# Decay tiles of the SSD part made during attention, B's convolution off TensorE, carry times decay on POOL

## The reference, cut to what matters

```python
xbc = silu(causal_depthwise_conv(xbc, conv_w, conv_b))       # 4 taps per channel, for x, B and C
xs, Bm, Cm = split(xbc)
a_cs = cumsum(dt * A, axis=2)                                # in chunks of 128 tokens
seg = a_t[..., :, None] - a_t[..., None, :]
decay = exp(where(causal, seg, -inf))                        # (chunk, group, head, 128, 128)
cb = einsum('bclgn,bcsgn->bcgls', Cc, Bc)
y_diag = einsum('bcgrls,bcsgrp->bclgrp', cb * decay, Xdt)
states = einsum('bclgn,bclgr,bclgrp->bcgrpn', Bc, decay_end, Xdt)
def step(carry, inp):                                        # over the chunks
    st, dec = inp
    return carry * dec + st, carry
y_off = einsum('bclgn,bcgrpn,bclgr->bclgrp', Cc, prev, exp(a_cs))
```

## Time and profile before

| | |
|---|---|
| median of 3 runs | 1903.23 us (1896.35 to 1906.76) |
| the profiled execution | 1899.2 us |
| its span, slowest core (7) | 1897.7 us (the cores: 1879.5 to 1897.7) |
| busy PE / DVE / ACT / POOL | 1797.5 / 1128.1 / 741.6 / 595.6 us |
| granted TensorE clock, core 7 | 0.988 |

### The profile page before, as it was taken

How to read it: one execution, slowest core, us unless ns; L and a number is a source line. 1 busy time by engine, 2 the same in 40 slices (tenths; PEclk the granted TensorE clock), 3 DMA queues, 4 the chain that set the end, 5 groups by cost and what they waited for, 6 DMA issues and landing times.

```text
span 1897.7 us, 35295 instructions; the slowest of 8 cores (1879.5 to 1897.7 us)
## 1 busy us (share of the span) xinstructions
PE 1797.5 (95%) x11590; PEld 998.2 (53%) x11590; DVE 1128.1 (59%) x2273; ACT 741.6 (39%) x1818; POOL 595.6 (31%) x730
## 2 busy tenths in 40 slices
PE   5999899999999888999999999999999999999996
PEld 2444455455445455666566656666566654444443
DVE  0134222222222435888988898888989887565565
ACT  1123433433344464555555555555555550000000
POOL 3000000000000103666765666666765660000000
PEclk9999999999999899999999999999999999999999
DMA  9919054441901511463738264453766574444341
GB/s 145 149 22 137 17 90 68 66 84 39 128 17 34 110 37 48 89 115 81 127 81 130 70 113 89 95 113 81 129 162 118 151 236 162 164 146 159 122 134 55
DMA packets 165460, 195.31 MB, mean 103 GB/s; under 512 B 96984, under 2 KB 123768, under 8 KB 158464
## 3 DMA queue, kind: packets, MB, share of 16 engines
q1 hardware_dynamic: 145888, 125.91, 26.1%
q0 software_dynamic: 19392, 67.15, 23.1%
HBM read 213.46 MB, written 42.22 MB: 135 GB/s over the span
## 4 chain that ended last, share of the span: by engine, by line
PE 71%; DVE 11%; DMA 8%; issue 5%; ACT 3%; POOL 1%; SPq 1%; DVEq 0%; ACTq 0%; POOLq 0%
PE bank L347 70%; DMA attst<-atg 3%; DMA vz_slab<-wpack 2%; DVE carry_r L363 2%; DMA slab<-wpack 2%; DVE cv_r L373 1%; DVE MT_r L363 1%; ACT tt L359 1%; ACT P L359 1%; DVE nrw_r L373 1%; DVE yn_r L373 1%; DVE t_r L363 1%; SPq L111 1%; DVE ss_r L368 1%; DVE carry_r L373 1%
## 5 line engine op out<-in xcount | busy, mean ns | idle before, releaser
L347 PE MATMUL bank<-xT_bf,slab 128*128 128x512 bf16 x2048 | 484.5, 382 | 20.6 <-DMA xT_bf<-xT 20.3
L347 PEld LDWEIGHTS bank<-xT_bf,slab 128*128 128x128 bf16 x2048 | 197.2, 99 | 233.2 <-issue 28.8
L347 PE MATMUL bank<-vz_slab,xT_bf 128*128 128x512 bf16 x1024 | 246.8, 384 | 9.2 <-DVE gz L373 6.7
L347 PE MATMUL bank<-w_out_bf,mb 128*128 128x512 bf16 x1024 | 234.7, 382 | 0.0
L347 PE MATMUL bank<-xT_bf,slab_r 128*128 128x512 bf16 x1024 | 234.1, 379 | 0.0
L359 ACT ACTIVATE dec_r<-abc_r,nb_tok 128x128 bf16<-128x128 f32 x512 | 204.7, 400 | 35.7 <-ACT dec_r L359 0.4
L363 POOL TENSOR_TENSOR t_r<-t_r,xd_r 128x256 f32<-128x256 f32 x120 | 102.4, 853 | 276.2 <-DVE t_r L363 274.1
L347 PEld LDWEIGHTS bank<-w_out_bf,mb 128*128 128x128 bf16 x1024 | 100.7, 99 | 122.1 <-issue 5.9
L363 POOL TENSOR_TENSOR abc_r<-abc_r,mask 128x512 f32<-128x512 f32 x128 | 159.8, 1249 | 9.0 <-DMA abc_r<-acs_d 8.4
L347 PEld LDWEIGHTS bank<-vz_slab,xT_bf 128*128 128x128 bf16 x1024 | 98.8, 99 | 116.8 <-issue 16.7
L347 PEld LDWEIGHTS bank<-xT_bf,slab_r 128*128 128x128 bf16 x1024 | 98.1, 98 | 106.7
(11 more groups left out here) (137 smaller groups left out, 2700.5 us busy)
## 6 DMA issues: line engine op xcount, KB each, us to landing
abc_r<-acs_d SPq DMA_DIRECT2D x128, 256.0 KB, 4.1
slab<-wpack POOLq DMA_DIRECT2D x20, 1024.0 KB, 12.7
xt<-x_tok SPq DMA_DIRECT2D x16, 1024.0 KB, 6.2
out<-xt SPq DMA_DIRECT2D x64, 256.0 KB, 2.3
wob<-w_out POOLq DMA_DIRECT2D x24, 512.0 KB, 25.0
slab_r<-wpack POOLq DMA_DIRECT2D x12, 1024.0 KB, 13.6
mb<-mixs SPq DMA_DIRECT2D x16, 768.0 KB, 5.2
xT_bf<-xT POOLq DMA_DIRECT2D x16, 512.0 KB, 44.6
```

The source lines that it names most:

```text
L347: return p.op("pe", lambda e: e.matmul(outap, lhsT, rhs, start=start, stop=stop), reads, writes, signal)
```

## The change

1. **Decay tiles.** From step 62 of the attention stage on, `dec_step` makes one of the 128 decay tiles after another: an SP DMA spreads a row of a_cs over the partitions into `dq` (three buffers), POOL adds the mask, VectorE adds the bias `nb_tok`, ScalarE takes one exponential over 512 columns into `dqo`, and an SP DMA stores it in DRAM (`dec_d`). 107 tiles are made by step 240, the rest by about step 312. The load of tile m + 3 follows the exponential of tile m. In the SSD stage `load_dec` brings each tile back four chunks ahead, into four buffers; `abc`, its masks and the four exponentials of `front` are gone.
2. **B's convolution.** For all blocks but the first, `conv_ew(2)` takes the place of `conv_fm(2)`: as C's, with one ScalarE and three VectorE instructions, issued within `proj(0)`. Both copies of `uT` that VectorE made (j = 0 and 2) go to ScalarE.
3. **Carry.** The product of carry and decay moves from VectorE, ahead of the addition, to POOL, behind the cast `prev_bf`, for the next chunk.
4. **Room.** `attst` has two buffers and not three; the new tiles lie on `dt_tok`, on the constants (`ones_bf` is set after step 256 by a memset) and on unused halves of `tt`.

```diff
@@ in the attention stage
+        def dq_of(i):
+            return i % 3 if i % 3 < 2 or i < DQ_TURN else 3
+        def dec_load(i):
             if i < 128:
+                k = dq_of(i)
+                p.dma("sp", [(dq[k][:, :], acs_d[i // 16, i % 16].rearrange("h l -> (h l)")
+                              .unsqueeze(0).to_broadcast([128, 512]))], "dq%d" % k, reads=[b_acsd], writes=[b_dq[k]])
+        def dec_add(i):
+            if i < 128:
+                k, g, c = dq_of(i), i // 16, i % 16
+                v = dq[k][:, :].rearrange("p (a b) -> p a b", a=4)
+                TT("pool", dq[k][:, :], dq[k][:, :], mask4_bf[:, :], ALU.add, [b_const], [b_dq[k]])
+                TT("dve", v, v, nb_tok[:, c, 4 * g:4 * g + 4].unsqueeze(2).to_broadcast([128, 4, 128]), ALU.add,
+                   [b_ssdc], [b_dq[k]])
+        def dec_out(i):
+            return i % 2 + (2 if i >= DQ_LAST else 0)
+        def dec_exp(i):
+            k, o_ = dq_of(i), dec_out(i)
+            ACT(dqo[o_][:, :], dq[k][:, :], AF.Exp, [b_dq[k]], [b_dqo[o_]])
+        def dec_store(i):
+            o_ = dec_out(i)
+            p.dma("sp", [(dec_d[i], dqo[o_][:, :])], "dqs%d" % o_, reads=[b_dqo[o_]], writes=[b_decd[i]])
...
+        DQ_START, DQ_LAST = 62, 107
+            goal = (i - DQ_START) * DQ_LAST // (240 - DQ_START) if i < 240 else DQ_LAST + (i - 240) * (128 - DQ_LAST) // 72
+            while ndq[0] < min(128, goal):
+                m = ndq[0]
+                ndq[0] += 1
+                dec_exp(m)
+                dec_store(m)
+                dec_load(m + 3)
+                dec_add(m + 1)
...
             E_act(i)
             if i % 2 == 1 and i < 60:
                 next(dtgen, None)
+            dec_step(i)
@@ SSD stage: gen_A
-                CPY("dve" if j % 2 == 0 else "act", uT[:, j, 3:515], banks[bk][:, :], [bkb[bk]], [b_uT[j]])
+                CPY("act", uT[:, j, 3:515], banks[bk][:, :], [bkb[bk]], [b_uT[j]])
...
-            yield from proj(0)
-            yield from conv_fm(2)
+            for i_, v in enumerate(proj(0)):
+                if i_ == 0 and Q > 0:
+                    conv_ew(2, cv2, b_cv2, BT[par][:, :], [b_BT[par]])
+                yield v
+            if Q == 0:
+                yield from conv_fm(2)
@@ front
             ACT(cb_bf[i2][:, :], banks[0][:, 0:128], AF.Copy, [bkb[0]], [b_cb[i2]], scale=0.25)
-            for hl in range(4):
-                ACT(dec_bf[i2][:, hl * 128:(hl + 1) * 128], abc[i3][:, hl * 128:(hl + 1) * 128], AF.Exp,
-                    [b_abc[i3], b_ssdc], [b_dec[i2]], bias=nb_tok[:, c, 4 * g + hl:4 * g + hl + 1])
@@ back_ew
-            if 0 < c < 15:
-                TT("dve", v4(carry[:, :]), v4(carry[:, :]), bc4(cd_bc[:, hs4, c]), ALU.mult, [b_ssdc], [b_carry])
...
             if c < 15:
                 CPY("act", prev_bf[:, :], carry[:, :], [b_carry], [b_prev])
+            if c < 14:
+                TT("pool", v4(carry[:, :]), v4(carry[:, :]), bc4(cd_bc[:, hs4, c + 1]), ALU.mult, [b_ssdc], [b_carry])
@@ the loop over n
-                load_abc(n + 5)
-                mask_abc(n + 3)
+                load_dec(n + 4)
                 back_ew(n)
```

More of the change, by code:

```diff
@@ L286, in make_cpack @@
     put("convbg", cbg)
-    cbc = np.zeros((128, 8, 5), np.float32)
-    for g in range(8):
-        ch = 3072 + g * 128 + np.arange(128)
-        cbc[:, g, 0:4] = conv_w[:, ch].T
-        cbc[:, g, 4] = conv_b[ch]
-    put("convbc", cbc.reshape(128, 40))
+    cbc = np.zeros((128, 2, 8, 5), np.float32)
+    for b in range(2):
+        for g in range(8):
+            ch = 3072 - 1024 * b + g * 128 + np.arange(128)
+            cbc[:, b, g, 0:4] = conv_w[:, ch].T
+            cbc[:, b, g, 4] = conv_b[ch]
+    put("convbc", cbc.reshape(128, 80))
     return cp
@@ L329, in build_program @@
     b_acsd = Buf("acs_d")
+    dec_d = nc.dram_tensor("dec_d", [128, 128, 512], BF16, kind="Internal").ap()
+    b_decd = [Buf("dec_d%d" % i) for i in range(128)]
     tot_d = nc.dram_tensor("tot_d", [32, 16], F32, kind="Internal").ap()
@@ L765, in build_program @@
         gz_tok = [RB.alloc([128, 4, 256], BF16, "gz_tok%d" % i) for i in range(2)]
-        abc = [RE.alloc([128, 512], F32, "abc%d" % i) for i in range(4)]
+        dec_bf = [RE.alloc([128, 512], BF16, "dec%d" % i) for i in range(4)]
+        dq.append(RE.alloc([128, 512], F32, "dq3"))
+        dqo += [RE.alloc([128, 512], BF16, "dqo%d" % i) for i in (2, 3)]
+        b_dq.append(Buf("dq3"))
         normw = [RA.alloc([128, 256], F32, "normw0"), RD1.alloc([128, 256], F32, "normw1")]
@@ L1326, in O_st @@
         def O_st(h, g):
-            a3 = (4 * h + g) % 3
+            a3 = (4 * h + g) % 2
             bm = Buf("mix")
```

103 lines of the change are left out of this document (64 added, 39 removed).

## The result

The kernel got slower. The changed kernel took 1930.8 to 1936.2 us, the kernel before 1896.35 to 1906.76; the ratio is 1.0165, 95% interval 1.0122 to 1.0207. Three of its six executions came in a slower state, in which the cores of one die show a lower granted clock; such executions are left out of every time and ratio in this document. The forecast was 1878, range 1850 to 1908: wrong, and on the wrong side. The profiled execution took 1930.96, its span 1929.4 against 1897.7.

What follows compares the result with a forecast made beforehand. The prediction took TensorE to bound the SSD stage, with VectorE close behind, and nearly fill attention. SSD -33.9 and attention +8.5 gave -25.4 us on the profiled 1899.2, 1873.8; with the median 4.0 higher, 1878 us, range 1850 to 1908.

Steps and rivals of the forecast that it cites:

- TensorE's matmuls in SSD: SSD stage: B's four matmuls leave TensorE in 31 of 32 blocks, 1.08 us each, -33.5 us.
- The -6.4 for `uT`: SSD stage: TensorE's waits for `uT` copies that VectorE made late go, as ScalarE makes them; -6.4 us.
- VectorE's burst: SSD stage: B's three taps come as a 3 us burst on a late VectorE; +6 us (-2.7 to +19).
- Both stay covered by TensorE's 25.3: nothing: SSD stage: less work on ScalarE and POOL gains nothing, both being covered by TensorE's 25.3 us a block.
- the third rival: Room on every engine: all TensorE's idle 14.6 us in SSD goes, attention comes out even; 1855 us, chance 0.17.
- it makes 7.4: no wait: Attention: a decay tile's loop from load to exponential takes 7.4 us at the usual 4.1 us landing, against 9.7 available.
- the +13 us for late tiles: Attention: tiles come late while six slabs load, 2.2 us each; +13 us (0 to 27).
- a gain of 7.5 us: Attention: masks spread the `wob` copies, so two waits of TensorE and their clock drops go; -7.5 us (to 0).
- -7.5 + 13 + 3: Attention: spread `wob` copies -7.5, late tiles +13, VectorE's wait for the first tile at step 62 +3 us.
- over 25: Sign against the forecast: attention losing over 25 us, or gaining at all.
- The second rival: Attention: the decay tiles' loop from SP's DMA to `dq` holds the stage, half the tiles late; 1929 us, chance 0.10.
- The last pair, +5 - 3 - 2 = 0: Last head pair: 21 tile exponentials partly seen +5; waits for `P` behind front's exponentials -3 and in a jam -2 us.

Runs made afterwards that it cites:

- conv_pe: The changed kernel with B's convolution back on TensorE and the `uT` copies for j = 0 and 2 back on VectorE; 1929.3 and 1935.3 us, ratio 1.0184.
- jobs_early: The changed kernel with the SSD stage's weight slab loads issued ahead of `back_ew`'s operations in POOL's queue; 1894.8 and 1897.9 us, no ratio.
- part1: The changed kernel with only the decay tiles: B's convolution on TensorE, two `uT` copies and carry's product on VectorE; 1923.4 to 1936.6 us, ratio 1.0165.
- both: The changed kernel with 17 `wob` copies moved into the SSD stage and slab loads issued ahead of `back_ew`; 1865.2 to 1867.0 us, ratio 0.9836.
- wob_late: The changed kernel with seven `wob` copies before the tiles start and 17 in the SSD stage; 1909.9 to 1917.1 us, ratio 1.0073.
- few_tiles: The changed kernel making only the first three decay tiles, which all SSD loads read in turn; 1883.8 to 1888.9 us, ratio 0.9898.
- both_240: The version both with all 128 tiles made before step 240, none in the last pair; 1893.9 to 1907.0 us, ratio 1.0000.
- wob_early: The changed kernel with all 24 `wob` copies issued by step 46, ahead of the tiles; 1971.2 to 2000.6 us, ratio 1.0421.

## Why the prediction was wrong, point by point

**TensorE's matmuls in SSD: right in mechanism and size.** -33.5 forecast, -37.1 measured (conv_pe to jobs_early), but only where the slabs are in time. The -6.4 for `uT` came, but mostly not from where the forecast had it: its waits fell from 8.9 to 3.7 us in part1, with the copies still on VectorE, and from 3.9 (conv_pe) to 1.1 (jobs_early) with the copies on ScalarE.

**VectorE's burst, +6 in a bound of -2.7 to +19: inside the bound, the value taken too high.** With the product on POOL, TensorE waits 0.2 us for `carry` and `prev` in 550 us of both: the term is about 0. The taps themselves became shorter; groups by form, 900 to 1500 us of after, in the columns of the earlier trace rows:
```profile
L376 DVE SCALAR_TENSOR_TENSOR cv_r<-uT_r,cwb,cv_r 128x512 f32<-128x512 bf16 x140 | 130.0, 929 | 29.1 <-ACT cv_r L362 19.0
...
L376 DVE SCALAR_TENSOR_TENSOR CT_r<-tt,cv_r 128x512 bf16<-128x512 f32 x23 | 23.0, 1000 | 0.0
...
L376 DVE SCALAR_TENSOR_TENSOR BT_r<-tt,cv_r 128x512 bf16<-128x512 f32 x24 | 16.6, 692 | 12.0 <-ACT tt L362 8.9 <-DVE MT_r L366 1.4
```
929 ns in place of 1035, with POOL 58% busy in 850 to 1532 in place of 66%; and `BT` from two SBUF tiles took 692 ns, not the 1177 that the earlier trace rows gave for `CT` and that the sum used. `CT` took 1000 in the same stretch, so two SBUF inputs alone don't set the time. The prediction weighed the Trainium skill (SBUF — State Buffer, Who interferes with whom), by which a VectorE instruction with two SBUF inputs contends with a POOL instruction that reads SBUF. The three times fit it, though no run here takes POOL's work away alone. The prediction reckoned that the term would be 0 by that rule, and it was.

**"Both stay covered by TensorE's 25.3: nothing": wrong by about 19 us.** part1 shows 24.1, of which 5.2 are the waits for `uT` that the forecast had booked elsewhere. TensorE's idle 17.9 us in SSD before hung mostly on those engines: 14.2 of them go, as the third rival (room on every engine) had it for this stage. That gain stayed hidden in the result, since the slabs took it.

**Slabs: missing from the sum.** The changed blocks use 1 MB slabs faster, and their loads stand in POOL's queue behind an addition that waits for VectorE. +24.3 us of waits, 34.9 in all. The prediction counted which queues the new issues pass, not how soon the old ones must be there when the stage speeds up. Together: 842.2 - 24.1 - 37.1 = 781.0, + 34.9 = 815.9.

**"it makes 7.4: no wait": the step that failed.** This is the lap of the decay tiles, and with it the +13 us for late tiles. The paragraph before it booked the spread of `wob` as a gain of 7.5 us, and a gain there was: waits for `gz` over the whole run fell from 6.7 to 1.3 us. The prediction did not carry the same spread into the lap, for which it took the median landing of the trace before, where the `wob` copies came in jams and nothing ran in a loop. Spread, they lie beside half of the tiles' loads: landing 5.0 (5.3 in 420 to 650), DMA share 0.79. The forecast's lap, 7.4 against 9.7, had 2.3 us to spare where no slab loads; the real one is 5.3 + 3.3 = 8.6 in the median at the least, without SP's transposes and without what stands in front on VectorE and ScalarE. So a load a little later than most passes 9.7, as the laps of 10.2 and 10.1 above do, and the lost time isn't made up. wob_late (landing 3.9, lap 7.2) is the forecast's case, and there step 240 is 3 to 13 us late on the slowest core, and 14 to 18 in the median, where the forecast's terms for this stretch make +8.5 (-7.5 + 13 + 3).
So some 21 us of the 36 in the median are the loop, which the forecast had at no wait outside slab loads. Of the other 15, 4 are there in few_tiles too, and 11 are the tiles' own work in the engines' queues, which the forecast had as covered. On the slowest core the term of +13 was some 40 us; four programs of the same attention code lie between 655.7 (part1) and 669.1 there. That this is a limit and not a price per operation is shown by both_240. By its own signs, too, the forecast was wrong: attention lost 60.8 us, where "over 25" was to refute it. And its range was too narrow for its terms: if all its bounds are added, they give 1846 to 1924, not 1858 to 1903.
The second rival had the mechanism and the place, at a chance of 0.10. That its time came out too (1929; measured 1930.8) is luck in part: it had half of the tiles landing above 6.4 us, where 26 of 104 did (11 to 24 on the other cores), and its sum had none of the 24 us of the last pair, 10 of which aren't the tiles', nor the two errors in SSD, a gain 27 us larger than forecast and 35 us of slabs, which largely cancel. Its own text had what should have raised its chance: 32 late tiles sufficed. And the change adds 384 KB of DMA for each tile to this stage.

**The last pair, +5 - 3 - 2 = 0: wrong by 24 us.** From last `kT` to last `PV` 89.8 us before, 113.4 after. 10 of them are there with few_tiles, whose tiles are not. POOL's queue at the start of the pair, first of before, then of few_tiles:
```profile
642.51 3.37 POOL L363 TENSOR_TENSOR abc_r<-abc_r,mask 128x512 f32<-128x512 f32 x3 [8.38 <-DMA abc_r<-acs_d]
645.84 0.57 POOL L111 DMA_DIRECT2D slab<-wpack  x1
```
```profile
632.94 0.54 POOL L111 DMA_DIRECT2D slab<-wpack  x1
```
The masks had kept this slab load and two more right behind it 13 us back. Without them the three start at once, together with SP's loads, and TensorE stands, in few_tiles:
```profile
660.45 0.59 PE L350 MATMUL bank<-vp,P 128*128 128x129 bf16 x4 [15.42 <-ACT P L362]
```
in place of the 4.05 us of the earlier trace rows; the granted clock in 650 to 660 was 0.51 there and 0.53 in before. That the burst of slabs makes the stall is read from these rows and was not tried by itself. The other 6 to 13 us of the pair (few_tiles 100.0, wob_late 106.3, both 109.4, after 113.4) come with the tiles. In both_240, which makes no tile in the pair, it takes 102.0, so most of it hangs on the 21 tiles made there; how it divides between their exponentials and their loads stays open.

**The sum, as it should have been (slowest cores):** attention +40 before step 240 and +24 behind it, less 3 around the start of SSD; SSD -24.1 - 37.1 + 34.9 = -26.3; tail -3. +31.7 us.

## What to carry to other kernels

A loop that runs through queues of several engines and a DMA is checked by its lap against its budget, and the landing in it must be that of the new traffic, not the median of a trace without it; half a microsecond per tile decided between 13 and 57 us (both and both_240; 14 and 53 by the medians). When a change both spreads transfers and adds a loop that waits for transfers, the gain and the price are one item. And where a stage is made faster, ask of every load in it whether it still comes in time: here moving an issue up in POOL's queue was worth 0.3% before the change and, with the copies moved out of the loop's way, turned a 1.65% loss into a 1.6% gain.

## What the runs showed of the hardware

- 24 copies of 512 KB from DRAM to DRAM, issued by POOL within 48 steps, made a store of 2 KB take 51.1 us to land, and TensorE wait 77.9 us for one `P` behind it (wob_early); spread over 240 steps (after) no wait for a `P` was longer than 11.4 us.
- The loads of POOL's queue hold the DMA engines long for their bytes. In 420 to 600 us of the changed kernel that queue, with eight such copies and two slabs, moved 6.87 MB for 23.2% of the 16 engines' time; SP's moved 22.27 MB for 53.7%, which is 3.4 against 2.4 points per MB.
- The product of `carry` took 773 ns in the mean on VectorE before, with a median of 419 over the whole stage and a longest of 1949, and 679 in the mean on POOL in the changed kernel; what its move was worth, 0 or 24 us, followed not from these two numbers but from what VectorE had to do beside it.
